# A float32 transformer kernel: the first block's attention, its projections and its weight slots rearranged

## The reference, cut to what matters

```
h   = concat(meta (16 tokens), x (512 tokens))
hn  = rms_norm(h)
proj = hn @ w_in      # q_a 512, k_a 128, v_a 128, q_b 512, k_b 512, v_b 512, f 8
o_a = sliding-window attention, 8 query heads on 2 key heads, T5 bias, sink logit
o_b = forgetting attention, 8 heads, causal, logit += cum[q] - cum[k]
h  += rms_norm(concat(o_a, o_b) @ w_out)
h  += rms_norm((silu(g) * u) @ w_down),  g, u = rms_norm(h) @ w_gate_up
```

## Time and profile before

| | |
|---|---|
| median of 3 runs | 2049.14 us |
| the profiled execution | 2045.14 us |
| its span | 2043.3 us |
| TensorE busy | 1860.3 us, 91% |
| VectorE busy | 1083.0 us, 53% |
| ScalarE busy | 731.9 us, 36% |
| GpSimd busy | 152.4 us, 7% |
| mean granted TensorE clock | 0.954 |

### The profile page before, as it was taken

The page is one execution under the profiler, slowest core; times in us unless marked ns, Lnnn a source line. Parts: engine busy times, 40 slices in busy tenths (PEclk is TensorE's granted clock), DMA queues, the critical chain, the costliest instruction groups (busy, mean ns, idle before and its releaser), DMA issues.

```text
span 2043.3 us, 22242 instructions
## 1 busy us (share of the span) xinstructions
PE 1860.3 (91%) x9011; PEld 1506.3 (74%) x9011; DVE 1083.0 (53%) x1779; ACT 731.9 (36%) x1171; POOL 152.4 (7%) x146
## 2 busy tenths in 40 slices
PE   4999999969999999499999999997689999999993
PEld 3888888738888788377778878876577778788772
DVE  6023776364455533554445876473464347967453
ACT  4023665422221222245543232341436432322422
POOL 3000000120011000110000000104100000000012
PEclk9799999989999999699999999999799989999996
DMA  4212000204555422122111222222122112222220
GB/s 165 70 63 103 2 1 2 83 31 148 183 205 196 175 89 97 62 83 83 62 62 62 103 83 104 94 92 82 42 83 83 63 41 90 96 101 85 84 82 41
DMA packets 29108, 177.53 MB, mean 87 GB/s; under 512 B 3565, under 2 KB 3709, under 8 KB 11726
## 3 DMA queue, kind: packets, MB, share of 16 engines
q1 hardware_dynamic: 20016, 144.71, 19.9%
q0 software_dynamic: 8608, 31.21, 4.4%
q10 hardware_dynamic: 382, 0.19, 0.0%
HBM read 171.28 MB, written 4.78 MB: 86 GB/s over the span
## 4 chain that ended last, share of the span: by engine, by line
PE 83%; DVE 9%; ACT 4%; POOL 2%; issue 1%; POOLq 0%; ACTq 0%; DVEq 0%
PE ps L538 26%; PE ps L540 24%; PE ps L539 24%; PE ps L871 2%; PE ps L546 2%; DVE R L1381 2%; DVE w_lo L1339 2%; POOL acc L454 2%; PE ps L856 1%; ACT w_hi L918 1%; ACT h L918 1%; PE ps L595 1%; PE ps L862 1%; DVE tmp L1346 1%; PE ps L704 1%
## 5 line engine op out<-in xcount | busy, mean ns | idle before, releaser
L538 PE MATMUL ps<-Xh,w_hi 128*128 128x512 f32 x1640 | 657.1, 401 | 59.7 <-DVE Xl L1339 43.2
L540 PE MATMUL ps<-Xh,w_lo 128*128 128x512 f32 x1640 | 645.6, 394 | 0.0
L539 PE MATMUL ps<-Xl,w_hi 128*128 128x512 f32 x1640 | 645.3, 393 | 0.0
L1339 DVE TENSOR_TENSOR w_lo<-w_raw,w_hi 128x2048 fp32r<-128x2048 f32 x134 | 310.6, 2318 | 265.2 <-ACT w_hi L918 265.2
L538 PEld LDWEIGHTS ps<-Xh,w_hi 128*128 128x128 f32 x1640 | 312.7, 191 | 138.2 <-issue 45.1
L539 PEld LDWEIGHTS ps<-Xl,w_hi 128*128 128x128 f32 x1640 | 312.8, 191 | 68.3 <-issue 4.3
L540 PEld LDWEIGHTS ps<-Xh,w_lo 128*128 128x128 f32 x1640 | 311.9, 190 | 66.5
L918 ACT ACTIVATE w_hi<-w_raw 128x2048 fp32r<-128x2048 f32 x134 | 256.1, 1911 | 121.9 <-DMA w_raw<-in_w 121.9
L1346 DVE SCALAR_TENSOR_TENSOR cacc<-ain,vec,cacc 128x512 f32<-128x512 f32 x240 | 161.9, 747 | 0.0
L918 ACT ACTIVATE gt<-ps 128x512 f32<-128x512 f32 x48 | 28.3, 597 | 201.8 <-PE ps L540 201.8
L595 PE MATMUL ps<-acc,ones 128*128 128x512 f32 x32 | 22.3, 786 | 77.8 <-POOL acc L454 65.7
(11 more groups left out here) (293 smaller groups left out, 2653.3 us busy)
## 6 DMA issues: line engine op xcount, KB each, us to landing
w_raw<-in_w SPq DMA_DIRECT2D x134, 1024.0 KB, 4.8
ada_w<-in_w_ada POOLq DMA_DIRECT2D x48, 512.0 KB, 4.5
bias_scratch<-brow POOLq DMA_DIRECT2D x2, 1312.0 KB, 5.5
h<-in_xT SPq DMA_DIRECT2D x4, 512.0 KB, 6.1
out<-h SPq DMA_DIRECT2D x1, 2048.0 KB, 6.3
bias<-bias_scratch POOLq DMA_DIRECT2D x1, 1024.0 KB, 6.3
bias<-bias_scratch POOLq DMA_DIRECT2D x1, 512.0 KB, 4.7
cact<-in_c POOLq DMA_DIRECT2D x1, 512.0 KB, 6.5
```

The lines of the kernel that those rows point to most:

```text
L538: nc.tensor.matmul(o_, whi, xhi, start=start, stop=False)
L539: nc.tensor.matmul(o_, whi, xlo, start=False, stop=False)
L540: return nc.tensor.matmul(o_, wlo, xhi, start=False, stop=stop)
L1339: return nc.vector.tensor_tensor(o_, a_, b_, op)
```

## The change

- Slots 1 to 12 are laid out anew (L1927 ff.): slots 3 and 4 hold all 512 columns of v_b for 4 of the 8 k-steps each, slots 5 and 6 q_b, 7 and 8 q_a; w_out is four slots, each with 4 k-steps by 4 tiles, the fox heads' rows first (slots 9, 10) and the window heads' rows after (11, 12).
- v_a is made like k_a (weights stationary, 512 tokens moving) and turned by four transposes. v_b is made with 512 moving columns in banks 2 to 5.
- All 8 `bias_rows` calls stand after the first tile of slot 0, between tiles of slots 0 and 1.
- At the start `ones` is set before `Qb` and `Kb` rows are; the squares of x are added up by VectorE instead of GpSimd.
- In attention scores and values are single float32 matmuls. All splits of q, k, v and `PT` are gone, as are the copies `out_read` and all `keep_busy` calls inside it. Scores use two pairs of banks.
- Attention starts after slot 5. The 80 k-steps of slots 6 to 10 stand between its steps: 4 ahead of unit 0, 12 over units 0 to 11, 64 over units 12 to 63. Sums of slots 9 and 10 are copied to `y1` and slots 11 and 12 added by VectorE.
- Slots 7 to 12 are split whole at units 3, 11, 20, 33, 46 and 57.
- Slot 13 is split at the begin of slot 11's tiles, by both engines ahead of their reads.

```diff
+S_Q2, S_QA, S_OF, S_OW = 6, 7, 9, 11
+DENSE_STEPS = KD * (Q2_TILES + QA_TILES) + 4 * OF_TILES
+def dense_until(u):
+    q2 = KD * Q2_TILES
+    if u < 0:
+        return FIRST_STEPS
+    if u < 12:
+        return FIRST_STEPS + (u + 1) * (q2 - FIRST_STEPS) // 12
+    return q2 + -(-(u - 11) * (DENSE_STEPS - q2) // (UNITS - 12))
+SPLITS = {u0 + 2: (g,) for u0, g in ((1, 7), (9, 8), (18, 9), (31, 10), (44, 11), (55, 12))}
...
             def scores(u):
-                if u >= 3:
-                    pe.wait_ge(pt_lo_done, u - 2)
+                if u >= 2:
+                    pe.wait_ge(pt_done, u - 1)
...
             for u in range(UNITS):
                 transposes(u)
+                dense(dense_until(u))
                 if u + 2 < UNITS:
                     scores(u + 2)
-                if u:
-                    values(u - 1)
-            values(UNITS - 1)
+                values(u)
...
 # ScalarE
             for u in range(UNITS):
                 if u + 1 < UNITS:
                     exp_unit(u + 1)
                 pt_unit(u)
+                for t in tiles_ended(u):
+                    dense_read(t)
+                if u in SPLITS:
+                    slot_hi(*SPLITS[u])
+                if u % (2 * NB) == 1 and u > 1:
+                    out_hi(u // (2 * NB) - 1)
...
 # VectorE
             for u in range(UNITS):
                 norm_unit(u)
...
                 if u + 1 < UNITS:
                     max_unit(u + 1)
-                if u:
-                    pt_lo_unit(u - 1)
+                if u in SPLITS:
+                    slot_lo(*SPLITS[u])
```

More of the change, by code:

```diff
@@ L599, in _, with bias_rows @@
             sums(0, KD)
[L600 to L614, removed]
+            def bias_rows(hd):
+                b = 4 + 2 * (hd % 2)
+                if hd >= 2:
+                    pe.wait_ge(brow_done, hd - 1)
+                for o_, c in ((bank(b, ROW_W), slice(0, ROW_W)), (bank(b + 1, ROW_M), slice(ROW_W, ROW))):
+                    nc.tensor.matmul(o_, tabb_hi[:, hd, :], onehot_r[:, c], start=True, stop=False)
+                    last = nc.tensor.matmul(o_, tabb_lo[:, hd, :], onehot_r[:, c], start=False, stop=True)
+                last.then_inc(brow_full, 1)
             pe.wait_ge(meta_sum, 1)
@@ new lines, in values, with dense @@
+                pe.wait_ge(pt_done, u + 1)
+                (fox_pv if hd < HEADS else swa_pv)(hd, b).then_inc(pv_done, 1)
+            q2_fills = [fills.f[b].val(1) for b in range(2)]
+            qa_fills = [fills.f[i % 2].val(2 + i // 2) for i in range(QA_TILES)]
+            done = 0
+            def dense(until):
+                nonlocal done
+                for i in range(done, until):
+                    tile, k, n, g, j = dense_step(i)
+                    if k == 0:
+                        pe.wait_ge(w_lo_done, g + 1)
+                        wait_fill(fills, tile % 2)
+                    if g < S_OF:
+                        whi, wlo = w(g, k * 2 * P + j * P)
+                        xh, xl = Xh[:, k, :], Xl[:, k, :]
+                    else:
+                        if tile == Q2_TILES + QA_TILES:
+                            pe.wait_ge(o_lo, k + 1)
+                        whi, wlo = w(g, k * T + j * P)
+                        xh, xl = oh[k], ol[k]
+                    last = mm3(bank(tile % 2), whi, wlo, xh, xl, k == 0, k == n - 1)
+                    if k == n - 1:
+                        last.then_inc(slot_done if j == (1 if g < S_OF else 3) else tile_full, 1)
+                done = until
@@ new lines, in _, with queries_read @@
+            tf.add(NB)
+            sc.wait_ge(slot_done, 5)
+            act_(Vm[0:NM, P:P + T], bank(0, T, 0, NM), ACT.Copy).then_inc(bank_read[0], 1)
+            def queries_read(hd0, b):
+                for e in range(2):
+                    last = act_(Qb[0:DH, hd0 + e, :], bank(b, T, DH * e, DH * (e + 1)), ACT.Copy, scale=-0.125)
+                last.then_inc(bank_read[b], 1)
+            slot_hi(6)
+            sc.wait_ge(rows_out, 1)
+            for j in range(2):
+                full(tf, 5, j == 1)
+                queries_read(2 * j, j)
@@ L1935, in _stream @@
     pair(w_in, qa + heads[2], qa + heads[3])
-    rows = np.concatenate(heads + [r(512, 512)])
-    for i in range(4):
-        pair(w_out[rows], r(256 * i), r(256 * i + 128))
+    rows = np.concatenate([r(512, 512)] + heads)
+    for r0 in (0, 512):
+        for half in range(2):
+            rows4(w_out[rows], r0, r(512 * half, 512))
     for t in range(KF):
```

581 lines of the change are left out of this document (279 added, 302 removed).

## The result

| | before | after |
|---|---|---|
| median of the runs, us | 2048.16 (2045.56 to 2049.57, 4 runs) | 2071.57 (2067.65 to 2075.07, 4 runs) |
| profiled execution: span, us | 2043.3 | 2071.8 |
| mean granted clock | 0.954 | 0.927 |
| first transposes to first transposes of the last unit, us | 162.34 | 253.92 |

The changed kernel is slightly slower: the ratio of its time to the time before is 1.0115, 95% interval 1.0092 to 1.0139, some 23 us. In later measurements some executions of the kernel before took 2078 to 2129 us at a lower clock; every ratio in this document leaves those out. The forecast was 2028.7 us, with a range of 1999 to 2046; the result is outside that range, on the other side.

A forecast was written before the change was run, and what follows sets the result against it. TensorE was taken to bound the kernel, busy over 98% of each long stretch. Terms 39.9 + 12.4 + 85.9 + 11.5 + 5.1 + 215 + 25.8 + 0.75 = 396.4 against 416.8, -20.4 from 2049.1: 2028.7 us, range 1999 to 2046.

The forecast's parts named there:

- Start, slot 0, slots 1 to 5, first scores: Before attention: first tile done at 39.9 us, then 12.4, 85.9, 11.5 and 5.1; attention begins at 154.8.
- The units without splits: Attention's 64 units: 184.4 us plus 1 for dense reads and output splits; fox head 11.6 to 12.0, window head 11.2.
- The splits: Six attention units with whole splits: TensorE idles 3.4 us and 4.2 us are lost at each, 25 us in all.
- The upper bound of 36: Upper bound on the loss at the six split units, with both splits in full: 36 us.
- The clock: At the six split units: after 3.4 us idle the clock may fall, half of six at 1.7 us, 5 us.
- Behind the units: Output projection after attention: 25.8 us for 46.0, with 3.2 us idle in it and part of a clock fall.
- the 0.75 counted: After the output projection: the last tile passes VectorE before its square, +0.75 us; later only places in SBUF change.
- rival 2: Attention units: clock falls because `keep_busy` is gone and TensorE waits in every unit; 22 falls, 2061 us; chance 0.10.
- the argument against it: Second block's float32 attention with dense work between keeps clock 1.00 wherever idle stays short; k-steps stand in every unit.

The follow-up runs named there:

- e12: Changed kernel with the splits of slots 7 to 12 cut to a sixteenth of their width, output wrong; 2009.65 us, ratio 0.9815.
- e11: Changed kernel with splits in quarters, low part one unit later, slot 13 one slot later, meta products among wide ones; 1998.63 us, ratio 0.9764.
- e2: Changed kernel, whole splits kept, 7 idle multiplications of 256 columns put in the gap at each of six split units; 2030.16 us, ratio 0.9917.
- e9: Changed kernel with splits in quarters and the first norm's eight squares added on GpSimd again; 2018.39 us, ratio 0.9860.
- e1: Changed kernel with six weight slots split in quarters over four units instead of whole at one; 2022.39 us, ratio 0.9867.
- e6: Changed kernel, whole splits kept, five k-steps per split moved behind the next unit's transposes, the gap left idle; 2054.65 us, ratio 1.0031.

## Why the prediction was wrong

On the axis of the span the forecast was 2043.3 - 20.4 = 2022.9, and 2071.8 was measured: 48.9 too little.

- *Start, slot 0, slots 1 to 5, first scores:* right, together 1.3 us off. One reason in it was wrong though its number was right: the start is 4.4 us faster (22.55 for 26.96) in spite of the additions on VectorE, which cost 1.8, not because of them.
- *The units without splits,* 185.4: 194.9 measured, 9.5 too little. A fox head takes 12.7 to 13.1 us in e12, not 11.6 to 12.0, a window head 11.4 to 11.5 for 11.2, but for two with small waits. It is not the chain over the other engines, since TensorE is hardly ever idle there: its own work was priced too low. The fifth fox head of e11 (13.05 us, no wait in it), counted from start to start, has 4.2 us of value products where 3.3 were forecast, 3.1 of scores for 2.7, and 4.5 for five k-steps at 0.68 (3.4); only its transposes were cheaper, 1.2 for 1.5.
- *The splits,* six times 4.2 = 25: 20.5 (212.91 less 192.41). Place, mechanism and the 3.4 us of idle as forecast. The upper bound of 36, "with both splits in full", does not follow: six times 1.91 and 2.32 is 25.
- *The clock,* "after 3.4 us idle the clock may fall; half of six at 1.7 us, 5": this is the step that failed. It fell at six of six, and a fall cost 6.8 us: 253.92 less 212.91 is 41.0 us, eight times the term. Of the 36 us missed, 5 come from counting three falls for six and 31 from the price. The 102 us at half clock agree. Units at half clock took some 1.7 times as long as at full clock, not twice (units 12 to 14: 16.27 us, for 9.47 in e2), and 102 us less 102/1.7 is 42, an estimate from these rows.
- *Behind the units:* right, 0.6 off. In the rest of the kernel 5.7 us more than the 0.75 counted; over the profiles of these runs that stretch took 1624 to 1633 us, and nothing in them was changed there. I have no cause for it.

The price of a fall was read from a place where it is cheap: behind 706.22 come dense short products, and the clock is back after 3.4 us. In the units it comes back after 12 to 22. The same 1.7 us went into rival 2, which had the right mechanism and the right sign; the granted clock of 0.79 over the units is under the 0.93 that was named as its mark. Its 2061 us, from a count of 22 falls, was too low and had the wrong make-up: not many cheap falls, but six dear ones. And the argument against it, that the second block keeps 1.00 wherever idle stays short, was true (1.00 from 920 to 1060 us of the trace before, with no wait there over 1.5 us) and did not bear on units with 3.4 us of idle, which the same text had just forecast.

The Trainium skill (TensorE: Matmul & The Clock Gate, "HAM oscillation") describes a loop in which a wait in every round brings the clock down each time, and advises to restructure it so that TensorE stays busy through the products before the next wait. The trace agrees for the split units, six of six, and the runs agree with the advice: quarters or a later low part take the wait away and the falls with it.

What stays open: what else than the wait's length decides whether the clock falls (2.68 us did not, 2.61 did; at unit 57 the same 0.91 us did in e9 and not in e1; behind 0.72 us it fell in thinner units), and what in a unit's work keeps it down. The dense burst of e6 brought it back sooner, but no run varied transposes, scores and value products one by one.

## What to carry to other kernels

Price an idle stretch of TensorE by the work that stands behind it: the same wait cost 3.3 us of idle and 6.8 us of low clock here, and 1.7 us of low clock where dense short products followed. An operation that waits for another engine's long half should stand behind the short ones that the next unit needs: two lines, the low part one unit later, were worth 59.5 us. A freeing of engines pays only when the order lets it: the change was 1% slower than before as written, and with its splits and narrow products placed otherwise 2.4% faster. And where TensorE is busy nearly all of a stretch, the first thing to check is the price of its own work: that alone was 9.5 us of the miss.

## What the hardware showed that I had not expected

- With whole splits the clock stayed at the level of 1.2 GHz for 12 to 22 us of unbroken TensorE work (34 matmuls in 12.2 us where 57 fit at full clock), and a burst of some six dense k-steps cut that to about 5 us at the fall at 205.6. Three units at half clock took 1.7 times their time at full clock, not twice.
- The same wait at the same place had opposite outcomes in two kernels that differ only in the start: 0.91 us at unit 57, 1.00 behind it in e1 and some 10 us at 0.50 in e9.
- 24 products of 16 columns in a row, behind the small products of the position bias, were enough for a fall with no wait at all (TensorE busy 30.00 of 30.00 us): 0.83 over 40:70, and 1.00 when each three stood behind three of 512 columns.
- GpSimd's additions made VectorE's small table operations 3.4 times as long (5.69 for 1.65 us), and the start was still 1.8 us faster with them there.
